# A fused two-layer block on one core: the v projection by seven products, loads in the order of the splits, and weight-block sums made by adding transfers

## The reference, cut to what matters

```
h  = rmsnorm(x, a_norm)                      # (256, 2048)
u, v, gate = split(h @ a_w_in, 3)            # three products of 2048 x 4096
v  = rmsnorm(gelu(v), v_gain)
y  = gelu(u) * (w_s per group @ v + b_s)
x1 = rmsnorm(x + (y * silu(gate)) @ a_w_out, final_norm)
...                                          # attention, mLSTM, merge, w_out
f  = silu(conv(g)) * conv(w)                 # (256, 5632)
out = x2 + f @ w_down                        # 5632 x 2048
```

## Time and profile before

| | us |
|---|---|
| median of 3 runs | 2128.38 (2125.08 to 2128.59) |
| the profiled execution: its own time | 2127.12 |
| its span in the profile | 2125.3 |
| busy: PE | 2116.2 |
| busy: DVE | 1313.1 |
| busy: ACT | 1045.8 |
| busy: POOL | 16.6 |

### The profile page before, as it was taken

One profiled execution on the slowest core, in us unless ns is written; L12 is line 12 of the kernel. 1 busy time (PEld: TensorE's weight loads), 2 busy tenths in 40 slices (PEclk: granted clock), 3 DMA queues, 4 the chain that ended last, 5 costly groups with the idle time before them and its releaser, 6 DMA issues.

```text
span 2125.3 us, 24874 instructions
## 1 busy us (share of the span) xinstructions
PE 2116.2 (100%) x10090; PEld 1771.0 (83%) x10090; DVE 1313.1 (62%) x1466; ACT 1045.8 (49%) x1220; POOL 16.6 (1%) x17
## 2 busy tenths in 40 slices
PE   9999999999999999999999999999999999999999
PEld 7888888888888887888888888888888888887887
DVE  5445566656555554554654555567777777779984
ACT  6445444444444444554454444455555555555552
POOL 0000000000000000100000000000000000000000
PEclk9999999999999999999999999999999999999999
DMA  8665566555755555544455565556556556554554
GB/s 303 197 195 172 189 203 204 191 193 179 253 188 188 188 197 170 177 150 149 149 187 190 187 196 186 185 176 189 188 182 195 192 183 194 182 189 178 219 219 157
DMA packets 111810, 404.37 MB, mean 190 GB/s; under 512 B 12496, under 2 KB 13264, under 8 KB 111312
## 3 DMA queue, kind: packets, MB, share of 16 engines
q1 hardware_dynamic: 109440, 394.66, 56.3%
q10 hardware_dynamic: 2256, 8.14, 1.0%
HBM read 400.65 MB, written 2.10 MB: 189 GB/s over the span
## 4 chain that ended last, share of the span: by engine, by line
PE 94%; DVE 4%; DMA 1%; ACT 1%; issue 0%; SPq 0%; ACTq 0%; DVEq 0%
PE g L409 61%; PE xs L428 8%; PE g L428 8%; PE g L693 5%; PE xs L432 4%; PE g L432 4%; DVE w_lo L1090 2%; PE xs L452 1%; DMA raw<-in_stream 1%; PE xs L714 1%; DVE block L1094 1%; PE xs L573 1%; PE g L714 1%; PE xs L481 1%; ACT w_hi L764 0%
## 5 line engine op out<-in xcount | busy, mean ns | idle before, releaser
L1090 DVE TENSOR_TENSOR w_lo<-raw,w_hi 128x1024 fp32r<-128x1024 f32 x719 | 877.5, 1224 | 758.7 <-ACT w_hi L764 755.2
L764 ACT ACTIVATE w_hi<-raw 128x1024 fp32r<-128x1024 f32 x719 | 760.9, 1059 | 956.2 <-PE g L409 643.5
L409 PE MATMUL g<-w_hi,in_both 128*128 128x512 f32 x1536 | 478.5, 391 | 3.3 <-DVE w_lo L1160 3.3
L409 PE MATMUL g<-w_hi,mid_both 128*128 128x512 f32 x1280 | 406.5, 393 | 0.0
L409 PEld LDWEIGHTS g<-w_hi,in_both 128*128 128x128 f32 x1536 | 289.7, 189 | 63.7 <-DVE in_both L1153 3.5
L409 PE MATMUL g<-w_lo,in_both 128*128 128x512 f32 x768 | 299.8, 390 | 0.0
L409 PEld LDWEIGHTS g<-w_hi,mid_both 128*128 128x128 f32 x1280 | 240.4, 188 | 49.6
L409 PE MATMUL g<-w_lo,mid_both 128*128 128x512 f32 x640 | 249.2, 389 | 0.0
L428 PE MATMUL g<-mlp_both,w_hi 128*128 128x512 f32 x704 | 176.7, 393 | 0.4 <-DVE xw L1449 0.4
L428 PE MATMUL xs<-mlp_both,w_hi 128*128 128x512 f32 x704 | 176.3, 392 | 0.0
L409 PEld LDWEIGHTS g<-w_lo,in_both 128*128 128x128 f32 x768 | 144.9, 189 | 29.7
(11 more groups left out here) (263 smaller groups left out, 2049.8 us busy)
## 6 DMA issues: line engine op xcount, KB each, us to landing
raw<-in_stream SPq DMA_DIRECT2D x719, 512.0 KB, 3.5
block<-in_stream SPq DMA_DIRECT2D x24, 512.0 KB, 5.4
x_first<-in_x_tokens ACTq DMA_DIRECT2D x1, 2048.0 KB, 9.8
gain_row<-in_gain_rows SPq DMA_DIRECT2D x8, 256.0 KB, 2.7
xt<-in_x_tokens ACTq DMA_DIRECT2D x1, 2048.0 KB, 8.3
xf<-in_x SPq DMA_DIRECT2D x3, 512.0 KB, 9.3
out<-xw ACTq DMA_DIRECT2D x3, 512.0 KB, 3.1
final_row<-in_final_rows ACTq DMA_DIRECT2D x1, 1024.0 KB, 13.3
```

Of the source, the lines that this page charges most:

```text
L409: ins = mm(G[buf][:, t, :], a[:, kt, at_t], w[:, slot, j * COLS:(j + 1) * COLS], start=(kt == 0 and n == 0), stop=(last and j == ROWS_PER_ ...
L764: activation(w_hi[:, n % RING, :], of[:], ACT.Copy).then_inc(hi_ready, 1)
L1090: v.tensor_tensor(w_lo[:, n % RING, :], of, w_hi[:, n % RING, :].bitcast(F32), ALU.subtract).then_inc(lo_ready, 1)
```

## The change

- **v by products.** Phase v becomes four groups of two column blocks. The first is plain; the other three do 2, 1 and 2 of their four turns by products (`WIDE_STEPS`). The same code (`wide_chunk`, `wide_product`) now serves both v and down. Two sums of rows of `h` are made during the first group (`SUMS_AT`).
- **The result of v.** For groups 1 to 3 DVE prepares the four own products (`own_products`) and adds them to the banks into `v_all` (`v_result`); ACT then applies gelu and sums squares block by block (`v_out`). The first two blocks are only copied at first (`v_taken`), since the scale is not there yet, and get their gelu at items 20 and 23. The long sums of squares at the phase's end go.
- **Sums by transfers.** The first two of a turn's four block sums are made by a transfer of POOL's queue that adds a second weight block from device memory onto the block that lies in the buffer (`sums_by_loading`). The transfer for product 5 waits until product 1's low part has been made. Signs change so that all four are additions. DVE keeps two.
- **Loads after splits.** Blocks rotate over three buffers (`buffer_of`), so that each buffer is refilled with the next turn's block as soon as the last split that reads it is done (`NEXT_IN_PLACE`), and SP's list follows the items one by one.
- **Start.** `WARM_UP` goes from 11 to 17. Some of the loads and the splits of x move a little later. In v the chunks of a group come as row pairs of two column blocks, so rows of x are needed at half the rate.

```diff
-WARM_UP = 11
+WARM_UP = 17
...
+WIDE_STEPS = {
+    "v": (((0, None), (1, None), (2, None), (3, None)),
+          ((0, 3), (1, 2)),
+          ((0, None), (1, 3), (2, None)),
+          ((0, 2), (1, 3))),
+    "down": (((3, None), (4, None), (8, None), (9, None), (5, 0), (6, 1), (7, 2), (10, None)),
+             ((3, 0), (4, 1), (5, 2), (6, None), (7, None), (8, None), (9, None), (10, None))),
+}
+SUM_TURNS = {"v": (3, 2), "down": (0, 1, 2)}
+SUMS_AT = {"v": (7, 10), "down": (7, 9, 11)}
...
+NEXT_IN_PLACE = {7: B11, 3: B12, 4: B22, 2: B21}
+def buffer_of(q, b):
+    return b if b == B21 else (b + q - quads_ahead(QUADS[q][0])) % 3
...
+            # SP
+            for n, item in enumerate(ITEMS):
+                if item.product in NEXT_IN_PLACE and quad_of(item) + 1 < len(QUADS):
+                    q = quad_of(item)
+                    if QUADS[q + 1][0] == item.phase:
+                        sp.wait_ge(lo_ready, n + 1)
+                        load_block(q + 1, NEXT_IN_PLACE[item.product])
+                if not item.product and CHUNK_COUNT[n] + RING < len(CHUNK_ITEMS):
+                    c = CHUNK_COUNT[n] + RING
+                    sp.wait_ge(lo_ready, n + 1)
+                    sp.dma_start(raw[:, c % RING, :], stream[stream_of(ITEMS[CHUNK_ITEMS[c]])]).then_inc(
+                        raw_full[c % RING], 16)
...
+            # ACT, high_of_chunk
+                    elif item.product == 5:
+                        act.wait_ge(sem["first_sum_in"], 16 * (uses + 1))
+                    elif item.product == 7:
+                        act.wait_ge(sem["side_sum_in"], 16 * (uses + 1))
...
+            def v_out(q):
+                act.wait_ge(group_read[q % 2], q // 2 + 1)
+                at_v = v_all[:, :, col_block(q)]
+                by_token(at_v, at_v, ACT.Gelu_apprx_tanh, scale).then_inc(sem["v_ready"], 1)
+                act.wait_ge(sem["v_ready"], q + 1)
+                for t in range(2):
+                    ins = activation(v_junk[:, t, :], at_v[:, t, :], ACT.Square, accum_out=v_ss[:, t, q:q + 1])
+                ins.then_inc(sem["v_sq_ready"], 1)
+                act.wait_ge(sem["v_sq_ready"], q + 1)
...
+                if n in (20, 23):
+                    if n == 20:
+                        act.wait_ge(sem["scale_ready"], 1)
+                    v_out((n - 20) // 3)
...
             # DVE, block_sums
-                if item.product == 1:
-                    dve.wait_ge(block_full[B11], 16 * uses)
-                    dve.wait_ge(block_full[B12], 16 * uses)
-                    dve.wait_ge(lo_ready, n + 1)
-                    block_sum(item, B11, B12, B11)
-                elif before and before.product == 1:
...
-                    block_sum(before, B12, B22, B12)
-                elif item.product == 5:
+                if item.product == 5:
+                    dve.wait_ge(block_full[B22], 16 * (quad_of(item) + 1))
                     dve.wait_ge(lo_ready, n + 1)
+                    block_sum(item, B11, B11, B22)
...
+            def v_result(q):
+                half = q % 2
+                dve.wait_ge(mm_done, half_end("v", q // 2, half) + 1)
+                to = v_all[:, :, col_block(q)]
+                by_t = ((v_wide.p1, v_wide.u_b), (v_wide.u_a, v_wide.u_d))[half]
+                for t in range(2):
+                    ins = v.tensor_tensor(to[:, t, :], GG[:, 2 * half + t, :], by_t[t][:], ALU.add)
+                ins.then_inc(group_read[half], 1)
...
+            # POOL
+            def sums_by_loading(uses):
+                phase, g, turn = QUADS[uses]
+                first, side = (wide[phase].blocks[buffer_of(uses, b)] for b in (B11, B12))
+                pool.wait_ge(block_full[B12], 16 * (uses + 1))
+                p.dma_start(side[:], stream[chunk_in_stream(phase, g, 1, 2 * turn + 1)],
+                            accum_op=ALU.add).then_inc(sem["side_sum_in"], 16)
+                pool.wait_ge(lo_ready, product_item(phase, g, turn, 1) + 1)
+                p.dma_start(first[:], stream[chunk_in_stream(phase, g, 1, 2 * turn)],
+                            accum_op=ALU.add).then_inc(sem["first_sum_in"], 16)
```

More of the change, by code:

```diff
@@ L105 @@
+FIRST_ITEM["end"] = len(ITEMS)
+ITEM_AT = {item: n for n, item in enumerate(ITEMS)}
+CHUNK_ITEMS = [n for n, item in enumerate(ITEMS) if not item.product]
 CHUNK_COUNT = {n: c for c, n in enumerate(CHUNK_ITEMS)}
+QUADS = [(item.phase, item.group, item.turn) for item in ITEMS if item.product == 1]
+GROUPS_BY_PRODUCTS = list(dict.fromkeys(quad[:2] for quad in QUADS))
 B11, B12, B22, B21 = range(4)
 PRODUCT_OF = {1: B11, 5: B11, 7: B12, 6: B11, 3: B22, 4: B11, 2: B21}
-LAST_USE = {B11: 4, B12: 7, B22: 3, B21: 2}
@@ new lines, in banks_of, with half_end, stream_of @@
+def banks_of(item):
+    if item.product:
+        return {RESULT_OF[item.product]} if item.product in RESULT_OF else set()
+    return {2 * item.half, 2 * item.half + 1}
+def half_end(phase, g, half):
+    return max(n for n, item in enumerate(ITEMS) if (item.phase, item.group) == (phase, g) and
+               banks_of(item) & {2 * half, 2 * half + 1})
+def stream_of(item):
+    if item.group is None:
+        return FIRST_CHUNK[item.phase] + item.row
+    return chunk_in_stream(item.phase, item.group, item.half, item.row)
@@ L367, in _ @@
                     sp.dma_start(gain_row[:, i % 2, :], gain_rows[i]).then_inc(sem[f"gain_in{i % 2}"], 16)
[L369 to L379, removed]
-                    row = 1 if b in (B22, B21) else 0
-                    sp.dma_start(blocks[b][:], stream[DOWN_AT + 22 * (2 * g + half) + 2 * i + row]).then_inc(
-                        block_full[b], 16)
-            sp.wait_ge(sem["out_ready"], 4)
+            sp.wait_ge(sem["out_ready"], 1)
             sp.dma_start(out[:, 0, col_block(3)], xw[:, 0, col_block(3)]).then_inc(sem["stored"], 16)
-            sp.wait_ge(sem["out_ready"], 6)
+            sp.wait_ge(sem["out_ready"], 3)
             sp.dma_start(out[:, 1, last_half(1)], xw[:, 1, last_half(1)]).then_inc(sem["stored"], 16)
@@ L460, in _, with opens @@
             pe.wait_ge(sem["first_half_lo"], 1)
-            for c in range(64):
-                if c in (1, 2, 4, 6):
-                    pe.wait_ge(sem["in_lo_ready"], 3 + c // 2)
-                one("v", c // 8, c % 8, tokens("v", c // 8, norm_in.hi, norm_in.lo))
+            opened = set()
+            def opens(item, bank):
+                key = (item.phase, item.group, bank)
+                new = key not in opened
+                if new:
+                    opened.add(key)
+                    _, _, read = group_of(item.phase, 2 * item.group + bank // 2)
+                    if read > 1:
+                        pe.wait_ge(group_read[bank // 2], read - 1)
+                return new
@@ new lines, in _ @@
+            for n in range(items_of("v")):
+                item = ITEMS[n]
+                if n:
+                    pe.wait_ge(lo_ready, n + 1)
+                    if item.half == 0 and item.group == 0 and item.row:
+                        pe.wait_ge(sem["in_lo_ready"], (3, 4, 4, 5, 5, 6, 6)[item.row - 1])
+                if item.product:
+                    if item.product == 1:
+                        pe.wait_ge(sem["sums_lo_ready"], sum_slot("v", item.turn) + 1)
+                    ins = wide_product(item, norm_in.hi, norm_in.lo, n % RING)
+                else:
+                    ins = wide_chunk(item, norm_in.hi, norm_in.lo, n % RING)
+                ins.then_inc(mm_done, 1)
@@ L1050, in _ @@
                         gate_tanh(i)
-            for n in range(len(DOWN)):
+            for n in range(items_of("down")):
                 if n == 0:
@@ L1613, in _ @@
             rstd(n_rstd[:, 0:2], n_ms[:, 0:2], "ms_ready", 4, "rstd_ready")
+            for uses in range(quads_ahead("down"), len(QUADS)):
+                sums_by_loading(uses)
 def chunks_of(w):
```

533 lines of the change are left out of this document (302 added, 231 removed).

## The result

The changed kernel takes **2190.57 us** (2184.03 to 2193.14, 4 runs), the kernel before on the same chip 2127.73 (2125.08 to 2128.59): ratio 1.0297, interval 1.0284 to 1.0309, so it is 3% slower. Predicted were 2123.3 us, with a range of 2116 to 2133. The profiled execution took 2192.2 us, its span is 2190.4.

A forecast was written before the change was run, and what follows sets the result against it. TensorE was taken to set the time. From 2127.12 us, 6.8 (matmuls), 2.4 (start) and 2.5 (down's waits) came off, then 5.8 (transfer wait) and 2.0 (gelus) were added: 2123.2, stated as 2123.3, range 2116 to 2133.

The forecast's parts named there:

- 5.8: Mixed quads: TensorE waits for the first sum's transfer, 0.96 us in each of six quads, nothing in five others.
- 2115.4: Whole kernel: forecast time in us after all three gains, before the new transfer wait and the gelus are added.
- the queues are nearly empty where it is issued: First sum's transfer: with loads spread out it lands after 4.4 us, 3.1 plus 1.3 for a second pass.
- The budget of 3.44 us: Six quads behind a mixed one: time from product 1's low part to the transfer's landing before TensorE is late.
- The budget of 6.16 us: Five quads behind a plain turn: time the transfer has to land, so these quads were to lose nothing.
- The start (2.4 us): Kernel start: longer warm-up keeps the fast clock through a hole of about 2 us, gaining 2.4 us.
- The matmuls (6.8 us): Phase v: five turns go from 48 matmuls to 42, removing 30 from TensorE's path, 6.8 us gained.
- Rival 4: Phase v: products save nothing because ACT and DVE bind there; 2130 us, chance 0.10 shared with another rival.
- Hidden, and at nothing: Mixed quads of v: DVE's new adds for own products and results fit behind other work, costing nothing.
- The gelus (2.0 us): Phase v, items 20 and 23: gelus within a mixed quad delay high parts, 1.2 plus 0.8 us lost.
- Down's waits (2.5 us): Phase down, six mixed quads: stalls behind products 1 and 5 go with fewer DVE sums and earlier loads, 2.5 us gained.
- Rival 2: POOL's transfers: far too late, through POOL's software or waiting for DVE, landing after 6.9 us; 2142 us, chance 0.22.

The follow-up runs named there:

- e1: The changed kernel with all four block sums of a turn back on VectorE, no transfers that add; 2132.69 us, ratio 1.0029.
- e9: e6 with down's row sums back at items 7, 9 and 11 and v's gelu of quarter 3 at item 53; 2121.98 us, ratio 0.9983.
- e12: e9 with only down's first four blocks issued later, after items 11 to 14 instead of 6, 7, 9 and 10; 2119.05 us, ratio 0.9963.
- e3: The changed kernel with the same two transfers as plain loads, without the addition, so the output differs; 2153.89 us, ratio 1.0126.
- e2: The changed kernel with only the side sum (for product 7) on VectorE, the first sum alone on POOL's queue; 2169.45 us, ratio 1.0199.
- e10: e9 with the first sum by an adding transfer again, in e7's order of items, the side sum on VectorE; 2124.48 us, ratio 0.9996.
- e7: The changed kernel with its transfers, a turn's items reordered so the first sum has about 8.9 us; 2148.07 us, ratio 1.0104.
- e6: e5 with five more orders changed (v's first result, x's load and squares, gelus, down's row sums, down's bank waits); 2122.88 us, ratio 0.9983.
- e4: The kernel before the change with only the longer warm-up, 17 matmuls in place of 11; 2126.04 us, ratio 1.0001.
- e5: e1 with v's finished results (v_result) taken on VectorE ahead of the low part of the same turn; 2126.62 us, ratio 1.0001.
- e11: e9 with down's loads issued from where they stood before the change; 2118.66 us, ratio 0.9970.

## Why the prediction was wrong

In the profiled execution's measure the prediction was 68.9 us short (2192.2 - 2123.3). The experiments take it apart, by spans (a profiled time is 1.8 us above its span): 53.7 for the transfers (59.5, where 5.8 stood); 8.4 for orders on DVE and ACT, nearly all in v (10.4 from e1 to e9, where 2.0 stood for the gelus); 3.6 for down's first block (e9 to e12); and 3.3 that e12 still lacks to 2115.4. That is 69.0. Each span is of one execution, and the changed kernel's four go from 2182.2 to 2191.3, so the first term could be some us smaller.

- **The step that failed: "the queues are nearly empty where it is issued", and so a landing after 4.4 us.** Shown: 8.9 to 9.7 us in the five quads where the side sum has 4.6 to 5.9 us to go when the first is issued; in the six others 5.2 to 5.7 in four, and 7.2 and 7.7 in two. Two things were wrong. The side sum isn't out of the way: SP has just issued loads, its first packet starts up to 4.5 us after its issue, and the first sum goes behind it. And an addition is not a second pass at 408 GB/s: it doubles the engines' time (e3) and adds 1.6 us even to a lone transfer. The earlier trace rows had a floor, 3.1, and a ceiling, 7.0, which counted one transfer and no queue. I priced two transfers each by itself and never asked where the second stands behind the first. The queue is not all: e2 has one landing of 9.2 us and e10 six of 8.7 to 10.1 with nothing ahead on POOL's queue, and what slows those isn't taken apart.
- **The budget of 3.44 us was right behind a mixed turn, but for 0.3 us.** It runs from product 1's low part, and POOL issues 0.29 us after that, which the sum left out. In quad 4, 0.29 + 9.07 - 3.44 is 5.92 of lateness, and the table has 4.82 + 1.10; in quad 1, 0.29 + 9.61 - 3.44 is 6.46, against 5.35 + 1.37, where the other 0.26 is the half clock under product 5. e7 tests it the other way: with 8.9 us of budget product 5 hardly waits.
- **The budget of 6.16 us behind a plain turn was wrong in two of five quads**, which were to lose nothing. It takes product 1's low part as ended 5.58 us before product 1 starts; the changed kernel has it 4.7 to 5.7 before in three quads, but 0.77 before in v's first and 0.56 in down's first. In v ACT squares x just ahead of that high part:

```profile
49.57 1.90 ACT L1004 ACTIVATE x_junk<-x_first 128x2048 f32<-128x2048 f32 x1
51.38 0.18 ACT L1004 ACTIVATION_READ_ACCUMULATOR x_junk<-x_first 128x1 f32 x1
51.46 1.05 ACT L893 ACTIVATE w_hi<-v_block 128x1024 fp32r<-128x1024 f32 x1
```

  The low part ends at 53.77, and TensorE starts product 1 at 54.54. In down DVE makes the row sums and low parts without a pause from 1950.9 on and ends product 1's low part at 1963.67. So a landing of 5.7 us, shorter than the 6.16 allowed, cost quad 0 of the table its 5.35 us, and both quads wait much as long in e2 (5.5 and 4.1 us). In e12, with e6's orders, v's first quad has the low part 5.58 us ahead, as the sum had it.
- **What was queued behind ACT's wait was named too narrowly.** I named the high parts. In v's first quad `v_taken(0)` stood there as well, which frees the bank of C0:

```profile
54.31 1.05 ACT L893 ACTIVATE w_hi<-raw 128x1024 fp32r<-128x1024 f32 x1
59.33 1.06 ACT L893 ACTIVATE w_hi<-v_block 128x1024 fp32r<-128x1024 f32 x1 [3.98 <-DMA v_block<-in_stream]
60.29 1.01 ACT L977 ACTIVATE v_all<-g 128x1024 f32<-128x1024 f32 x1
```

  That is PE's wait of 5.4 us for `v_all`, in that first quad. v lost 25.8 us to the transfers, not two quads' 1.9.
- **The clock.** It was counted for the start alone. After each of the changed kernel's ten longest waits (2.1 to 5.4 us of idle time) the matmuls have a pitch of 427 ns for a while, 1.2 GHz. The length of the wait alone doesn't tell this: before the same product 5, of v's second quad, e2 waits 3.64 us and its clock stays at 1.00, and at ug e1 waits as long as the changed kernel (2.14 us) without it. Behind a late product 5 of down this adds 0.5 to 0.9 us to the wait, before item 18 of v 2.5, and behind the banks opened late 1.5 and 1.8.
- **The start (2.4 us)** was right in its outcome: the clock stays at 1.00 and the first real matmuls keep the fast pitch. But in the changed kernel the hole of 2 us through which it was to live wasn't there: the fast clock came at 5.73 and not at 4.06, the warm-up ended at 7.34, and the first real matmul came at 7.48. In e1 the warm-up ended at 6.6, near the 6.4 predicted, the hole was 1.2 us, and the clock lived through it. e4 gained 1.9 us up to the first spatial matmul; the time of the whole kernel did not show it.
- **The matmuls (6.8 us)**: 30 went, as said, and e12's span, with the same count, is 8.4 us below that of before. Rival 4 fell in its reason: v by products is not bound by DVE or ACT, but orders of theirs in it cost more than those 6.8 us, 10.4 by spans.
- **"Hidden, and at nothing" for the new DVE work was wrong** in one place: `v_result` is short (0.68 each), but it frees a bank and stood behind a low part. In e1 TensorE waits 2.39 + 2.30 us at the two places, with slow matmuls behind the first (behind both in the changed kernel). Taken first, in e5, it still costs 1.24 + 1.16.
- **The gelus (2.0 us)**: in e1, 0.95 us before product 2 of v's first quad against 1.2 predicted, 0.5 in the next against 0.8. Right in place, and near in size.
- **Down's waits (2.5 us)**: the last five quads do lose their waits in e1, but there are new ones ahead of and in the first, 0.5, 0.74 and 0.61 us before items 684, 686 and 688, and 1.14 before item 673, for a bank. e11, where one wait of 0.5 us is left in down, tells that the gain did not come from loads behind the splits, since it has them not; what it has from the change is the buffers that rotate, and that they did it is not shown by itself.
- Rival 2's price (2142) was for a landing of 6.9 us, and its reason, that POOL's instruction waits for DVE, no run shows: POOL's issue takes 0.86 to 1.00 us each time, with DVE busy 62% of the span. By the Trainium skill, DMA: Bandwidth & Descriptors (Anatomy of one DMA — SWDGE (gpsimd) path), the estimate was 3.2 us; e3 measures 3.5 to 3.7 in four quads for a plain transfer with no other on POOL's queue, and 4.9 and 5.0 in two, so the rule nearly holds at best. The additions and the second transfer of a pair took longer, as above.

## What to carry to other kernels

A transfer moved into a chain of dependencies is priced from its issue to its landing behind everything that is on its queue at that moment, and an adding one at double the engine time. Then choose the item order for that latency: the same transfers cost 42 us less three items later. For each wait that is added, list all that the waiting engine does next, results that free a bank above all, and put those first; the same holds for a load's wait on a queue that feeds other items. Here plain additions on a VectorE that was busy 62% were better than any arrangement of transfers that was run.

## What the runs showed of the hardware

- An adding transfer of 512 KB with no other on its queue: 5.2 us to landing at best where a plain one takes 3.5 to 3.7 (but 8.7 to 10.1 in six quads of e10); 22 of them take 2.8% of the engines where the plain take 1.4%, and one takes 0.86 us on POOL to issue where the plain takes 0.53.
- Two of them in a row land one behind the other: 9.6 us for the second.
- The granted clock fell to 0.50 after 5.2 us without a matmul, and six matmuls later it was back. After waits of 1.8 to 3.6 us it was at 0.50 in some executions and at 1.00 in others: 3.53 us in the changed kernel and 3.64 in e2, before the same product. In the start, a hole of 0.14 us after 34 warm-up matmuls left it at 1.00, and one of 1.2 in e1.
